# Block 1 of a two-model float32 network on Trainium2: order of the first loads, of the state-space sums and of the output products

## The reference

```
u    = rmsnorm(x, norm_mix)
proj = u @ w_in                       # 1024 -> 512 (state space) + 3*512 (q, k, v)
y_ssm: per group g of 32, complex state x_t = Abar x_{t-1} + Bbar u_t, 64 states
       y_t = Re(C x_t) + D u_t;  y = gelu(y);  y = y * sigmoid(y @ w_glu + b_glu)
y_attn: stick-breaking attention, 8 heads of 64
gates = sigmoid(u @ w_gate + b_gate)
h = x + (g_ssm*(y_ssm @ w_up_ssm) + g_attn*(y_attn @ w_up_attn)) @ w_out
h = h + relu(rmsnorm(h) @ w_ff1)**2 @ w_ff2
```

## Time and profile before

| | us |
|---|---|
| median of 3 runs | 1690.17 (1689.16 to 1690.76) |
| the profiled execution, its time | 1691.35 |
| its span in the profile | 1689.6 |
| PE busy / PE weight loads busy | 1627.6 (96%) / 1381.5 (82%) |
| DVE busy | 1110.5 (66%) |
| ACT busy | 828.2 (49%) |
| POOL busy | 49.7 (3%) |
| mean granted clock of TensorE | 0.989 |

### The profile page before, as it was taken

The page is one execution under the profiler, slowest core; times in us unless marked ns, Lnnn a source line. Parts: engine busy times, 40 slices in busy tenths (PEclk is TensorE's granted clock), DMA queues, the critical chain, the costliest instruction groups (busy, mean ns, idle before and its releaser), DMA issues.

```text
span 1689.6 us, 24642 instructions
## 1 busy us (share of the span) xinstructions
PE 1627.6 (96%) x9690; PEld 1381.5 (82%) x9690; DVE 1110.5 (66%) x1480; ACT 828.2 (49%) x1077; POOL 49.7 (3%) x58
## 2 busy tenths in 40 slices
PE   6999899999999999999999999999999999999997
PEld 5876697888788888887888888788889877978886
DVE  5976766666766568865576655856577765665556
ACT  5455745343454346655454434634355655454443
POOL 1330100000000000000000000000000000000001
PEclk9998999999999999999999999999999999999999
DMA  7521343555655655532345556455664513454652
GB/s 205 159 66 51 100 142 122 196 179 194 215 174 174 199 199 149 176 101 75 125 150 174 183 189 209 166 172 186 211 193 132 175 51 100 150 173 154 205 188 100
DMA packets 206812, 264.53 MB, mean 157 GB/s; under 512 B 14106, under 2 KB 176276, under 8 KB 206740
## 3 DMA queue, kind: packets, MB, share of 16 engines
q1 hardware_dynamic: 206548, 263.50, 48.3%
q10 hardware_dynamic: 192, 0.04, 0.0%
HBM read 262.47 MB, written 1.05 MB: 156 GB/s over the span
## 4 chain that ended last, share of the span: by engine, by line
PE 86%; DVE 9%; ACT 2%; SPq 1%; issue 1%; DMA 0%; ACTq 0%; DVEq 0%
PE bank L445 41%; PE bank L484 21%; PE bank L486 11%; DVE wl L412 3%; PE bank L1612 2%; PE bank L1639 2%; PE bank L1205 1%; PE bank L1625 1%; ACT wh L405 1%; PE bank L679 1%; DVE wl L431 1%; PE bank L812 1%; DVE norm_small L731 1%; PE bank L1194 1%; PE bank L1640 1%
## 5 line engine op out<-in xcount | busy, mean ns | idle before, releaser
L484 PE MATMUL bank<-u_parts,wh 128*128 128x512 f32 x1664 | 590.6, 399 | 1.5 <-DVE u_parts L775 1.0
L412 DVE TENSOR_TENSOR wl<-raw,wh 128x2048 fp32r<-128x2048 f32 (+2 forms) x228 | 510.1, 2241 | 114.3 <-ACT wh L405 111.2
L405 ACT CAST wh<-raw 128x2048 fp32r<-128x2048 f32 (+3 forms) x235 | 437.2, 1864 | 89.5 <-PE bank L445 80.5
L486 PE MATMUL bank<-u_parts,wl 128*128 128x256 f32 x1664 | 467.0, 281 | 0.0
L484 PEld LDWEIGHTS bank<-u_parts,wh 128*128 128x128 f32 x1664 | 312.6, 188 | 79.4 <-issue 1.9
L486 PEld LDWEIGHTS bank<-u_parts,wl 128*128 128x128 f32 x1664 | 314.2, 189 | 1.9
L445 PE MATMUL bank<-u_parts,wh 128*128 128x256 f32 (+1 forms) x1344 | 257.3, 292 | 8.1 <-ACT tmp L1427 6.3
L445 PEld LDWEIGHTS bank<-u_parts,wh 128*128 128x128 f32 (+1 forms) x1344 | 212.0, 194 | 12.9 <-ACT tmp L1427 6.5
L445 PE MATMUL bank<-u_parts,wl 128*128 128x256 f32 (+1 forms) x672 | 192.0, 286 | 0.0
L445 PE MATMUL bank<-wh,hh 128*128 128x512 f32 x448 | 179.0, 400 | 6.6 <-DVE wl L412 4.5
L445 PE MATMUL bank<-wl,hh 128*128 128x512 f32 x448 | 174.7, 390 | 0.0
(11 more groups left out here) (340 smaller groups left out, 2036.2 us busy)
## 6 DMA issues: line engine op xcount, KB each, us to landing
raw<-ffn_wg SPq DMA_DIRECT2D x44, 1024.0 KB, 5.8
raw<-ffn_wu SPq DMA_DIRECT2D x44, 1024.0 KB, 5.3
raw<-ffn_wd SPq DMA_DIRECT2D x44, 1024.0 KB, 5.0
raw<-w_ff SPq DMA_DIRECT2D x32, 1024.0 KB, 5.3
raw<-w_in SPq DMA_DIRECT2D x28, 1024.0 KB, 5.6
raw<-w_out SPq DMA_DIRECT2D x12, 1024.0 KB, 5.0
raw<-w_gate SPq DMA_DIRECT2D x8, 1024.0 KB, 5.6
raw<-w_in SPq DMA_DIRECT2D x16, 512.0 KB, 5.4
```

The costliest lines, as they stand in the source:

```text
L405: ins = act.copy(dst, src)
L412: ins = dve.tensor_tensor(dst, src, upper.bitcast(F32), ALU.subtract)
L484: pe.matmul(two(bank[b + f]), slab_view(wh, slot, KD, WCOLS)[:, k, f * P:(f + 1) * P], u_parts[:, k, :, :], start=k == 0, stop=False, skip ...
L486: mm = pe.matmul(bank[b + f][:, 0:T], slab_view(wl, slot, KD, WCOLS)[:, k, f * P:(f + 1) * P], uh[:, k, :], start=False, stop=k == KD - 1, ...
```

## The change

- SP issues slabs 0, 1 and 2, then the state-space loads (before slab 3), and the vectors of block 2 before slab 5 instead of before slab 2. Those vectors land in a place of their own (rows_later).
- PE begins with 20 empty matmuls (KC0), turns the first half of x before the vectors, and the vectors between the halves, where the eight empty matmuls were.
- The turning of the parameter matrices moves behind step 4, the wait for the output matrices behind step 5, that of block 2's vectors behind step 6, with DVE's copies of them in step 7. Phase set 1 is finished by ACT in step 3 instead of step 1, and prepared by DVE after the split of slab 3.
- Tile 0 moves from step 5 to step 6, with tile 1. The input products of a step's tiles are all made at the end of the step before, interleaved (real parts of both, then imaginary parts of both); so the pair waits until both tiles of the present step have left banks 0 and 1.
- Output products of two tiles are interleaved, matmul by matmul. There are four product buffers instead of two.
- On DVE the split comes first in a step, then the step's first state, then dve_y, then the second state.

```diff
@@ -73,7 +73,7 @@
 
 SLABS1 = FF1 // (2 * P)
 SLABS2 = FF2 // (2 * P)
-KC1, KC2 = 8, 10
+KC0, KC1, KC2 = 20, 8, 10
 
 
 def shape_tables():
@@ -229,6 +229,7 @@
         stat = sb("stat", [P, 2, T])
         rstd = sb("rstd", [P, T])
         gates = sb("gates", [P, 2 * KD, T])
+        late_prod = sb("late_prod", [P, 2, 4, T])
         shared = sb("shared", [P, 4096])
         small = sb("small", [P, 4096])
         tables = sb("tables", [P, 2560])
@@ -663,10 +664,12 @@
         CLOCK_BANK = {j: 3 if j in (1, 4, 7) else 5 for j in range(8)}
         CLOCK_BANK_2 = {j: 7 if j in (1, 4, 7) else 5 for j in range(8)}
 
-        def big_pe(pe, j):
+        def big_pe(pe, j, meanwhile=None):
 
             for tt in range(NTT):
-                if tt == 1:
+                if tt == 1 and meanwhile is not None:
+                    meanwhile()
+                elif tt == 1:
                     keep_clock(pe, KC1, CLOCK_BANK[j])
                 for k in range(KD):
                     if k == 0:
@@ -858,6 +861,7 @@
         gflat = gates[:, :, :].rearrange("p a t -> p (a t)")
         flat = lambda t: t[:, :, :].rearrange("p a t -> p (a t)")
         rows_in = flat(act_out)
+        rows_later = small[:, 3584:3840]
         b_nat = [gflat[:, 2048 + 256 * i:2304 + 256 * i].rearrange("p (s c) -> p s c", c=16) for i in range(2)]
         b_bar = [gflat[:, 2560 + 256 * i:2816 + 256 * i].rearrange("p (s c) -> p s c", c=16) for i in range(2)]
         b_diag = [gflat[:, 3072 + 512 * i:3584 + 512 * i].rearrange("p (s c) -> p s c", c=32) for i in range(2)]
@@ -875,6 +879,7 @@
             buf, at = ((shared, 0), (shared, 2048), (gflat, 2048), (shared, 0))[i]
             return buf[:, at + which * 1024:at + which * 1024 + 1024].rearrange("p (j t) -> p j t", j=4)
         prod = [small[:, i * 1024:(i + 1) * 1024].rearrange("p (a t) -> p a t", a=4) for i in range(2)]
+        prod += [late_prod[:, i, :, :] for i in range(2)]
         ATT = 3 * P
         at_abs, at_pos, at_sp, at_w = (small[:, 2048 + ATT * i:2048 + ATT * (i + 1)] for i in range(4))
         merged = small[:, 0:2048].rearrange("p (k t) -> p k t", k=KD)
@@ -892,9 +897,9 @@
             "cd_in")
 
 
-        tiles_at = {5: [0], 6: [1], 7: [2, 3], 8: [4, 5], 9: [6, 7], 10: [8, 9], 11: [10, 11], 12: [12], 13: [13],
+        tiles_at = {6: [0, 1], 7: [2, 3], 8: [4, 5], 9: [6, 7], 10: [8, 9], 11: [10, 11], 12: [12], 13: [13],
                     14: [14, 15]}
-        PHASES_AT = {1: [0, 1], 5: [2], 11: [3]}
+        PHASES_AT = {1: [0], 3: [1], 5: [2], 11: [3]}
         NSTEP = 16
 
         def used_by(n):
@@ -965,7 +970,7 @@
                         src = src.rearrange("(s g) p -> s (g p)", g=2)
                     else:
                         src = src.rearrange("(k p) -> k p", p=P)
-                    sp.dma_start(rows_in[r0:r0 + src.shape[0], (1 + l) * P:(2 + l) * P], src).then_inc(vec2_in, 16)
+                    sp.dma_start(rows_later[r0:r0 + src.shape[0], l * P:(l + 1) * P], src).then_inc(vec2_in, 16)
             for l in range(LAYERS):
                 for i, nm in enumerate(("cmp_k_w2_2", "cmp_v_w2_2")):
                     for d in range(2):
@@ -975,9 +980,9 @@
             for tt in range(NTT):
                 sp.dma_start(res_tok[:, tt, :], a["x"][0].rearrange("(a p) d -> p a d", p=P)[:, tt, :]).then_inc(x_in[tt], 16)
             for n in range(N_FFN1):
-                if n == 1:
+                if n == 3:
                     ssm_loads(sp)
-                if n == 2:
+                if n == 5:
                     later_vectors(sp)
                 sp_slab(sp, n)
             n0 = N_FFN1
@@ -1054,7 +1059,6 @@
         N_VEC2 = 16 * LAYERS * len(ROW2)
 
         def b1_pe_start(pe):
-            pe.wait_ge(consts, 9)
             pe.wait_ge(vec_in, N_VEC)
             pe.transpose(bank[0][:, 0:ROWS1], rows_in[0:ROWS1, 0:P], ident[0:ROWS1, 0:ROWS1])
             pe.wait_ge(prep_dve, 1)
@@ -1063,7 +1067,7 @@
         def b1_pe_vec2(pe):
             pe.wait_ge(vec2_in, N_VEC2)
             for l in range(LAYERS):
-                mm = pe.transpose(bank[7][:, P * l:P * l + ROWS2], rows_in[0:ROWS2, P * (l + 1):P * (l + 2)],
+                mm = pe.transpose(bank[7][:, P * l:P * l + ROWS2], rows_later[0:ROWS2, P * l:P * (l + 1)],
                                   ident[0:ROWS2, 0:ROWS2])
             mm.then_inc(vec2_t, 1)
 
@@ -1087,9 +1091,6 @@
             TT = lambda o, x, y, op: link(dve.tensor_tensor(o, x, y, op))
             lre, lim = vec1[:, ROW1["A_re"]:ROW1["A_re"] + ST], vec1[:, ROW1["A_im"]:ROW1["A_im"] + ST]
             dve.wait_ge(zeroed, len(b_diag + c_t) + 1)
-            dve.wait_ge(vec2_t, 1)
-            for l in range(LAYERS):
-                link(dve.tensor_copy(vec2[:, l, :], bank[7][:, P * l:P * l + ROWS2]))
             link(dve.tensor_scalar(half_b[:, :], vec1[:, ROW1["b_gate"]:ROW1["b_gate"] + 2 * KD], 0.5, None, ALU.mult))
             dve.wait_ge(prep_act, 1)
             TT(col(ADT), lre, col(DT), ALU.mult)
@@ -1098,9 +1099,10 @@
             dve.tensor_tensor(col(FRAC), col(TURNS), col(WHOLE), ALU.subtract).then_inc(prep_dve, 1)
             dve_split(dve, N_IN1 + 2)
             dve.wait_ge(ssm_in, 16 * 7)
-            for i in range(2):
-                dve_phase(dve, i)
+            dve_phase(dve, 0)
             dve_split(dve, N_IN1 + 3)
+            dve_phase(dve, 1)
+            dve_split(dve, N_IN1 + 4)
             dve.wait_ge(prep_act, 2)
             TT(col(ARE), col(DECAY), col(COS1), ALU.mult)
             link(dve.tensor_scalar(col(ARE), col(ARE), 1.0, None, ALU.subtract))
@@ -1129,8 +1131,11 @@
                 for g in range(2):
                     ins = dve.tensor_copy(b_diag[i][64 * g:64 * g + 64, :, 16 * g:16 * g + 16], b_bar[i][64 * g:64 * g + 64, :, :])
                     ins.then_inc(bt_in, 1)
-            dve_split(dve, N_IN1 + 4)
             dve_split(dve, N_IN1 + 5)
+
+        def b1_dve_turned(dve):
+
+            link = lambda ins: chain(dve, dve_n, dve_chain, ins)
             dve.wait_ge(bt_taken, 1)
             for i in range(2):
                 link(dve.tensor_copy(b_t[i], bank[i][:, :].rearrange("p (i m) -> p i m", i=4)))
@@ -1185,25 +1190,32 @@
             chain(act, act_n, act_chain, act.activation(s, s, ACT.Sin, scale=2 * PI))
             act.activation(c, c, ACT.Sin, scale=-2 * PI, bias=quarter[:, 0:1]).then_inc(ph_done, 1)
 
-        def pe_bu(pe, s):
-            i, j = s // 4, s % 4
-            if s >= 2:
-                pe.wait_ge(bu_free, s - 1)
-            pe.wait_ge(lin_free[i // 2], 1)
-            r = slice(32 * j, 32 * j + 32)
-            pe.matmul(bank[s % 2][:, 0:T], b_t[0][r, i, :], us[r, i, :], start=True, stop=True)
-            pe.matmul(bank[s % 2][:, T:2 * T], b_t[1][r, i, :], us[r, i, :], start=True, stop=True).then_inc(bu_done, 1)
-
-        def pe_y(pe, s):
-            i, j = s // 4, s % 4
-            if j == 0 and i >= 1:
-                pe.wait_ge(y_taken, i)
-            pe.wait_ge(prod_done, s + 1)
-            p = prod[s % 2]
+        def pe_bu(pe, pair):
+
+            for s in pair:
+                if s >= 2:
+                    pe.wait_ge(bu_free, s - 1)
+                pe.wait_ge(lin_free[s // 8], 1)
+            for part in range(2):
+                for s in pair:
+                    i, j = s // 4, s % 4
+                    r = slice(32 * j, 32 * j + 32)
+                    mm = pe.matmul(bank[s % 2][:, part * T:(part + 1) * T], b_t[part][r, i, :], us[r, i, :], start=True, stop=True,
+                                   skip_group_check=True)
+                    if part == 1:
+                        mm.then_inc(bu_done, 1)
+
+        def pe_y(pe, pair):
+            if pair[0] % 4 == 0 and pair[0] >= 4:
+                pe.wait_ge(y_taken, pair[0] // 4)
+            pe.wait_ge(prod_done, pair[-1] + 1)
 
             for n, (c, q) in enumerate(((0, 0), (1, 3), (2, 2), (2, 1))):
-                mm = pe.matmul(bank[3][32 * j:32 * j + 32, 0:T], c_t[c][:, s, :], p[:, q, :], start=n == 0, stop=n == 3)
-            mm.then_inc(y_done, 1)
+                for s in pair:
+                    j = s % 4
+                    mm = pe.matmul(bank[3][32 * j:32 * j + 32, 0:T], c_t[c][:, s, :], prod[s % 4][:, q, :], start=n == 0, stop=n == 3)
+                    if n == 3:
+                        mm.then_inc(y_done, 1)
 
         def dve_state(dve, s):
 
@@ -1224,9 +1236,9 @@
             decay = col(DECAY)[:, s:s + 1].to_broadcast([P, T])
             dve.tensor_tensor_scan(act_out[:, 0, :], decay, stat[:, 0, :], 0.0, ALU.mult, ALU.add)
             link(dve.tensor_tensor_scan(act_out[:, 1, :], decay, stat[:, 1, :], 0.0, ALU.mult, ALU.add))
-            if s >= 2:
-                dve.wait_ge(y_done, s - 1)
-            p = prod[s % 2]
+            if s >= 4:
+                dve.wait_ge(y_done, s - 3)
+            p = prod[s % 4]
             dve.tensor_tensor(p[:, 0:2, :], act_out[:, :, :], cos2, ALU.mult)
```

(37 more changed lines are left out.)

## The result

| | before | after |
|---|---|---|
| median of the runs, us | 1690.65 (20 runs, 1688.91 to 1694.76) | 1692.4 (20 runs, 1691.34 to 1697.39) |
| the profiled execution / its span, us | 1691.35 / 1689.6 | 1692.8 / 1691.1 |
| start of the product after step 15, us | 209.5 | 211.8 |
| mean granted clock of TensorE | 0.989 | 0.982 |

The ratio of after to before is 1.0015, with an interval of 1.0008 to 1.0022: 1.75 us slower by the medians, less than the 0.2% that counts as a difference. The forecast was 1686.2 with a range of 1680.5 to 1693.5. The range holds the result, the sign is missed. Lines of the file moved: L405, L412, L1194/L1195, L1205 and L1219/L1220 of before are L406, L413, L1203, L1216 and L1231/L1232 of after.

The account below looks back on a forecast made before the run. SP's loads bound the start, mutual waits of PE and DVE steps 8 to 11, then PE alone. With 0.8 lost by step 11 and 4.8 won after, 4.0 less gave 1687.35 profiled, 1686.2 as median; range 1680.5 to 1693.5.

Parts of the forecast that it names:

- Part 1: Start to step 7: first waits go, POOL's phase set 2 is late next; step 7 at 75.3, 1.4 earlier.
- PE's long gap: End of step 6: PE stands 12, from 61 to 73, released by DVE's turning of state 1.
- The phase set: POOL's phase set 2, from about 47.6: 12.0 to 13.6 long, taken as 12.0 with DVE idle then, ending at 59.6.
- Part 2: Steps 7 to 11: a closing loop makes steps 8 to 10 equal, hardly shorter; step 11 at 141.3, 0.8 behind.
- The loop: Steps 8 to 10: scores, ACT's softplus and round, DVE's split, first state, turning, input products, values, scores; 17.1, 16.0, 16.4.
- The sum: Steps 8 to 10: loop terms, each split at 2.2, plus half clock of 1.9 and 2.65; 54.05 in all.
- the remainder of step 13: In the loop of steps 8 to 10: input products, values and scores together, taken as 2.65 (1.9 in step 8).
- Part 3: Steps 11 to 15, PE the bound: alternated outputs save 0.9 x 3, paired input products 1.05 x 2; 4.8 together.
- Sum: Whole kernel: 0.8 behind by step 11, then 4.8 won, so 4.0 less: 1687.35 profiled, 1686.2 as median.
- Fewer half-clock stretches: Rival: gaps of steps 8 and 10 might keep the clock, 2.65 for one, shorter phase set 1: 1682.5; chance 0.27.
- Input products that don't overlap: Rival, steps 6 to 10 and 13: each pair costs 2.1, or 4.2 at half clock: 1692.5 to 1695.6; chance 0.15.
- The loop eats all: Rival: half clock in all of steps 7 to 11, or late phase set and vectors: 1688 to 1690.5; chance 0.22.

Follow-up runs that it names:

- e5_yseq: The changed kernel with the output products of two tiles made one after the other again, not alternated; median 1697.72 us, ratio 1.0042 to the kernel before.
- e10_oldloads: The changed kernel with SP's state-space loads before slab 1 and vectors of block 2 before slab 2, as of old; 1700.46 us, ratio 1.007.
- e13_clock2: The changed kernel with 40, 31 and 56 empty matmuls filling PE's gaps in steps 8, 9 and 10; 1687.74 us, ratio 0.9983.
- e2_pool: The changed kernel with the three parts of POOL's phase set 3 ahead of the head's sum instead of behind it; 1689.01 us, ratio 0.9999.

## Why the prediction was right and wrong

**Part 1 was right in mechanism and within 0.8.** Steps 1 to 4 run without a gap, the matrices are turned at 44.8 (near 45.5 forecast), POOL begins at 46.8 (47.6), PE's long gap ends at 73.7 (73.1) and is released by the turning of the second state, step 7 starts at 75.7 (75.3), step 8 at 87.9 (87.3). Two terms inside were off. The phase set took 13.1, not 12.0: "DVE has nothing to do then" was wrong, the split of slab 7 runs from 55.33 to 57.62, and POOL's last part, begun at 55.84, takes 4.01. In e5_yseq, where that split was over at 56.16, the same part, from 56.18, took 2.40, and the products behind the gap came 1.3 earlier. The 13.1 was made up by the earlier start. And PE waits 3.0 for the tables at 52.3 (not forecast), after which the clock is down until 62.0 and step 6 slow; it ends at 65.5 instead of 61, hidden under the same gap. e10_oldloads puts the start's gain at 8.1.

**Part 2 failed, and it is nearly the whole miss.** Forecast for steps 8, 9, 10 with half clock: 19.0, 16.0, 19.05, step 11 at 141.3. Measured: 19.1, 19.5, 21.2, step 11 at 147.8. The loop was read rightly (step 8 is within 0.1), but two terms were left out of it.
- Half clock in step 9. The forecast charged it for steps 8 and 10 "and not for step 9, in whose gap the slow slab itself is taken up". The clock was down from 120.0 to 130.2, over its input products, values and scores. By the chain they take 2.08, 1.47 and 1.59 there, where full clock gives 1.13, 0.80 and 0.85: 2.35 of the 3.5 that step 9 is over. e13_clock2 agrees, 53.5 for the three steps with the clock kept.
- POOL beside DVE's split. The sum had 2.2 for every split; they took 2.35, 2.97 and 4.33. That is the rest of step 9's excess but 0.4, and 2.1 of the 2.15 by which step 10 is over. e2_pool removed it, and with it the half clock over step 9's input products, so the two terms are not independent.

A third slip is small: the remainder of step 13 after 5.93, 1.13 and 1.84 is 2.70, not 2.65.

**Part 3 was right in what the change saves, and in its sum by some luck.** From the start of step 11 to the product after step 15 I had 64.2, and it is 64.0. Step 11 is 12.8 where the sum has 14.1, mostly because its slab, which begins at half clock in both kernels, took 7.25, not the 8.37 of before. Steps 12 and 15 are each 0.7 longer than the sum has them: PE stands 0.50 at 167.05 for POOL's sum and 0.52 at 202.38 for DVE's products, and both waits were left out. Alternated outputs take 1.85 (1.9 taken), 0.9 less than in e5_yseq. A pair of input products takes 1.13 at full clock (1.05 taken).

**Sum.** By the profiles, step 11 is 6.5 later than forecast, the product after step 15 6.3, the whole 5.4 (1692.8 against 1687.35); the rest of the program was 0.8 shorter than before, which no part of the change explains.

**Rivals.** Fewer half-clock stretches: false, there were more. Input products that don't overlap: false by the 1.13. "The loop eats all": nearest, its half clock in all of the steps came, but its 1688 to 1690.5 lacked POOL's 2.7. It said "no change", and that was the outcome. My chance of 0.22 for it was too low: the sum rested on one of three like gaps keeping the clock, and I had seen both gaps of before lose it.

**What the change is made of**, by medians: DVE's order 10.4 faster (in the kernel before), the loads 8.1 faster, alternated outputs 2 to 5 faster, input products in pairs 19.5 slower. These don't add to 1.75: the first is measured where no loop stands in the way. The empty matmuls ahead of step 0, phase set 1 in step 3 and the four product buffers were not tried alone.

## What to carry to other kernels

Before work is paired, write down the loop that the pair closes (who must finish what before the pair may start) and sum it: here a pair saved PE 1 us and tied every step to ACT's round, DVE's split, a whole state and back. A gain elsewhere in such a step is only seen once the loop is no longer the longest thing. When a step shifts, look at what then runs beside what, on DVE and POOL above all, and charge the half clock to every gap of a kind of which one has already cost it.
